# Two low parts of a tuned two-stack kernel, moved behind the fifth pair's maxima and the compressed softmax's first half

## The reference, cut to what matters

```python
def first_block(...):
    for l in range(DEPTH):                       # DEPTH = 2
        proj = h @ w_in[l]
        mixed = concat([nsa_mixer(...), gla_mixer(...), pool_mixer(...)])
        h = layer_norm(DEEPNORM_ALPHA * h + mixed @ w_out[l], ln1_g[l], ln1_b[l])
        ff = square(relu(h @ w_up[l])) @ w_down[l]
        h = layer_norm(DEEPNORM_ALPHA * h + ff, ln2_g[l], ln2_b[l])
```

## Time and profile before

| what | value |
|---|---|
| median of three runs | 1451.93 us |
| profiled execution, its own time | 1452.05 us |
| its span | 1450.3 us |
| TensorE busy | 1398.2 us, 96% of the span |
| VectorE busy | 1056.3 us, 73% |
| ScalarE busy | 833.0 us, 57% |
| GpSimd busy | 526.8 us, 36% |
| mean granted TensorE clock | 0.991 of full speed |

### The profile page before, as it was taken

One profiled execution on the slowest core, in us unless ns is written; L12 is line 12 of the kernel. 1 busy time (PEld: TensorE's weight loads), 2 busy tenths in 40 slices (PEclk: granted clock), 3 DMA queues, 4 the chain that ended last, 5 costly groups with the idle time before them and its releaser, 6 DMA issues.

```text
span 1450.3 us, 29999 instructions
## 1 busy us (share of the span) xinstructions
PE 1398.2 (96%) x12859; PEld 1182.3 (82%) x12859; DVE 1056.3 (73%) x1361; ACT 833.0 (57%) x1253; POOL 526.8 (36%) x421
## 2 busy tenths in 40 slices
PE   8999999999999999999999999999999999999997
PEld 6778888888778888878678788887777778888886
DVE  5897986567797874567786888766667765898853
ACT  5575554336664453456885665545566777575552
POOL 0143995131057990234211366401212202146620
PEclk9999999999999999999999999999999999999998
DMA  9434466545243665525235455552533233556550
GB/s 369 172 117 146 146 211 214 189 168 181 87 145 114 233 205 202 189 88 189 94 134 209 140 200 177 189 193 88 175 116 118 88 106 118 199 187 205 188 178 30
DMA packets 35717, 235.61 MB, mean 162 GB/s; under 512 B 4736, under 2 KB 6784, under 8 KB 8832
## 3 DMA queue, kind: packets, MB, share of 16 engines
q1 hardware_dynamic: 35584, 233.68, 46.9%
HBM read 232.62 MB, written 1.05 MB: 161 GB/s over the span
## 4 chain that ended last, share of the span: by engine, by line
PE 74%; DVE 15%; ACT 7%; issue 2%; DMA 2%; SPq 0%; DVEq 0%; ACTq 0%
PE psum L690 23%; PE psum L692 22%; PE psum L691 22%; DVE low L2144 4%; PE psum L778 2%; DVE arena L2534 2%; ACT high L1538 2%; DMA raw<-stream 2%; ACT m L1891 1%; DVE m L2602 1%; DVE arena L2254 1%; DVE arena L2605 1%; ACT arena L2028 0%; ACT L2025 0%; DVE u L2445 0%
## 5 line engine op out<-in xcount | busy, mean ns | idle before, releaser
L2144 DVE SCALAR_TENSOR_TENSOR low<-raw,high 128x2048 f16<-128x2048 f32 (+4 forms) x246 | 528.1, 2153 | 251.8 <-ACT high L1538 251.6
L690 PE MATMUL psum<-u,high 128*128 128x272 f16 (+3 forms) x2136 | 589.9, 276 | 14.8 <-DVE u L2445 5.5
L691 PE MATMUL psum<-u,high 128*128 128x272 f16 (+3 forms) x2136 | 589.5, 276 | 0.0
L692 PE MATMUL psum<-u,low 128*128 128x272 f16 (+3 forms) x2136 | 589.4, 276 | 0.0
L1538 ACT ACTIVATE high<-raw 128x2048 f16<-128x2048 f32 (+4 forms) x246 | 420.0, 1711 | 139.1 <-PE psum L692 125.7
L690 PE MATMUL psum<-arena,high 128*128 128x256 f16 (+2 forms) x1264 | 346.7, 274 | 2.8 <-ACT arena L1876 1.5
L691 PE MATMUL psum<-arena,high 128*128 128x256 f16 (+2 forms) x1264 | 346.6, 274 | 0.0
L692 PE MATMUL psum<-arena,low 128*128 128x256 f16 (+2 forms) x1264 | 346.6, 274 | 0.0
L690 PEld LDWEIGHTS psum<-u,high 128*128 128x128 f16 (+1 forms) x2136 | 210.0, 98 | 53.0 <-issue 15.7
L691 PEld LDWEIGHTS psum<-u,high 128*128 128x128 f16 (+1 forms) x2136 | 210.1, 98 | 31.2 <-issue 0.7
L692 PEld LDWEIGHTS psum<-u,low 128*128 128x128 f16 (+1 forms) x2136 | 210.0, 98 | 30.6
(11 more groups left out here) (331 smaller groups left out, 1498.7 us busy)
## 6 DMA issues: line engine op xcount, KB each, us to landing
raw<-stream SPq DMA_DIRECT2D x208, 1024.0 KB, 4.8
raw<-stream SPq DMA_DIRECT2D x8, 768.0 KB, 4.1
raw<-stream SPq DMA_DIRECT2D x3, 896.0 KB, 4.9
con<-consts SPq DMA_DIRECT2D x1, 1758.0 KB, 16.5
raw<-stream SPq DMA_DIRECT2D x3, 512.0 KB, 3.4
h<-x_t SPq DMA_DIRECT2D x2, 512.0 KB, 6.1
out_t<-h SPq DMA_DIRECT2D x4, 256.0 KB, 2.1
misc<-small SPq DMA_DIRECT2D x1, 512.0 KB, 13.3
```

What stands on the lines that cost most here:

```text
L690: pe.matmul(out, w_hi, x[0], start=start, stop=False)
L691: pe.matmul(out, w_hi, x[1], start=False, stop=False)
L692: return pe.matmul(out, w_lo, x[0], start=False, stop=stop)
L2144: tell(dve.scalar_tensor_tensor(low[:, at:at + w], raw[:, off:off + w], W_SCALE, high[:, at:at + w], ALU.mult, ALU.subtract), split_ready ...
```

## The change: what it does

Five calls of VectorE's program for a layer are reordered. Before: weigh(3), low_part(13), maxima(4), low_part(14), first half of the compressed softmax, weigh(4), maxima(5), second half, weigh(5), give(9). After: weigh(3), maxima(4), first half, weigh(4), low_part(13), maxima(5), second half, weigh(5), low_part(14), give(9). No other engine's program is changed, and no instruction changes its operands. Pairs are counted from 0, so maxima(4) are those of the fifth pair.

```diff
--- before.py
+++ after.py
@@ -2370,9 +2370,7 @@
                 tell(dve.scalar_tensor_tensor(h15, t15, 1.0, h15, ALU.add, ALU.mult), hid_gated)
                 give(8)
                 weigh(3)
-                low_part(matrices[f"cmp_{l}_0"] + SPLIT)
                 maxima(4)
-                low_part(matrices[f"cmp_{l}_1"] + SPLIT)
 
                 dve.wait_ge(cmp_scored, l + 1)
                 s15 = sc[:, :, 0:CMP_N]
@@ -2388,6 +2386,7 @@
                 tell.settle()
                 tell(dve.tensor_tensor(s15, s15, along(sc_s[:, 1, :], CMP_N), ALU.subtract), cmp_shifted)
                 weigh(4)
+                low_part(matrices[f"cmp_{l}_0"] + SPLIT)
                 maxima(5)
                 dve.wait_ge(cmp_exped, l + 1)
                 tell(dve.tensor_reduce(sc_s[:, 2, :], s15, AX_X, ALU.add))
@@ -2404,6 +2403,7 @@
                 tell.settle()
                 tell(dve.tensor_tensor(s15, s15, along(sc_s[:, 0, :], CMP_N), ALU.mult), cmp_ready)
                 weigh(5)
+                low_part(matrices[f"cmp_{l}_1"] + SPLIT)
                 give(9)
 
                 def gate_gla(i):
```

## The result

The changed kernel takes 1462.47 us (median of 6), the kernel before 1452.01 (6): ratio 1.0076, 95% interval 1.0065 to 1.0086, so 10.5 us slower. The profiled execution took 1467.02 us, the slowest of the six. A second profile of the same kernel, from an execution of 1464.61 us (experiment 1), stands beside it further down.

A forecast was written before the change was run, and what follows sets the result against it. TensorE holds 74% of the chain, VectorE 15%, with the operand chain ending 0.1 us ahead of TensorE; 1452.05 + 4.0 (layer 0) + 4.6 (layer 1) = 1460.65, median 1460.5, likeliest range 1458.4 to 1462.9, 8-in-10 range 1452.2 to 1464.5.

The forecast's parts named there:

- the likeliest case: Both layers: L2931 gets in ahead of gate_gla(0) at full clock; 1460.5 us, range 1458.4 to 1462.9, chance 0.62.
- the sum: Whole kernel: 1452.05 + 4.0 (layer 0) + 4.6 (layer 1) = 1460.65 us; median 0.12 lower, so 1460.5.
- The low parts themselves: Low parts 13 and 14 on VectorE, ending near 101 and 109: no wait for slots 13 and 14, cost nothing.
- Up to maxima(5): VectorE, layer 0: maxima(5) starts at 101.0 against 102.21, 1.2 us earlier; in layer 1 about 0.6 earlier.
- TensorE loses both waits: Layer 0: the waits for weigh(4) (0.88 us) and cmp_ready (0.50) vanish in the best case; pooled_out ends at about 109.8.
- Stretching beside GpSimd: VectorE beside GpSimd's pooling: at best low(13)'s extra 0.85 us disappears, at worst softmax and weighing take 1.3 us more.
- L2931 ahead of gate_gla(0): L2931, issued at about 109.8 during low(15), precedes gate_gla(0); the first L2413 lasts 3.8 us instead of 0.42.
- The prediction's limit of "about 112": Layer 0: L2931 misses gate_gla(0) only if issued after about 112, with TensorE later than before.
- The size of the collision: VectorE is stopped 3.4 us at gate_gla(0) per layer; by the skill page's wording, 2.2 us more per layer.
- Operand chain: From gate_gla(0) to the output product's tile 0: later by 4.0 us in layer 0, 4.6 in layer 1.
- TensorE waits in several pieces for L2170: TensorE waits for L2170 in several pieces, about 4 us, inside the first output pair.
- The clock: Rival 1: collision plus half clock in one layer, 1.7 to 3.4 us; about 1463, up to 1464.5, chance 0.16.

The follow-up runs named there:

- experiment 1: The changed kernel again, with no edit, for a second profile: 1463.43 us against 1452.35 for the kernel before, ratio 1.0074.
- experiments 2 and 3: L2931 as a memset, scaled residual left out: in the changed kernel 1454.58 us, ratio 1.0014; in the kernel before 1452.15 us, ratio 0.9996.
- Experiment 5: The changed kernel with GpSimd also waiting for gate_gla(1) before it issues L2931: 1457.27 us against 1451.85 for the kernel before, ratio 1.0036.
- 7: The kernel before with low(14) alone moved, from behind maxima(4) to behind weigh(5): 1460.97 us against 1451.85, ratio 1.0063.
- experiment 4: The changed kernel with 40 TensorE matmuls into an unused bank between values(5) and the output product: 1460.15 us, ratio 1.0050.

## Why the prediction was right, and where its sizes were off

Forecast 1460.5, measured 1462.47, in the range. The direction and the mechanism were those of the likeliest case, a collision of L2931 with the head of the operand chain. The range held with some luck, because the sum left out a term that the two profiles show at 3.5 and 4.0 us. By its steps:

- *The low parts themselves*: right. They end at 103.6 and near 111, and the product starts at 122.35. ScalarE's waits for raw loads sum to 13.2 us over the whole program, as before.
- *Up to maxima(5)*: from weigh(3) it was to start 11.0 us on (12.2 before). It took 12.4 in the first profile (103.50), whose scores(4) are late, and 10.1 in layer 0 of the second; in layer 1 12.1 and 12.3, where I expected 11.6. The step depends on when scores(4) arrive against weigh(3), and a single profile hid it.
- *TensorE loses both waits*: wrong. The wait for weigh(4) went. The one for cmp_ready grew from 0.50 to between 1.8 and 2.5, because TensorE got there 2 to 4 us earlier, while cmp_ready itself, which stands behind low(13) and maxima(5), came only 0.8 to 2.1 us earlier. pooled_out comes 0.1 to 0.8 us earlier against weigh(3), not 1.5. (The two waits sum to 1.38, so by its own figures the prediction had pooled_out end at 110.0 and not 109.8.)
- *Stretching beside GpSimd*: of the right kind. In the first profile low(13) took 2.82 instead of 3.13 and L2394 0.17 instead of 1.15, and others took longer instead (L2263 1.10 in layer 0, L2265 2.30 in layer 1). In layer 0 of the second L2394 is back at 1.15.
- *L2931 ahead of gate_gla(0)*: right in three of the four layers of two profiles, with 3.86 us against the 3.8 named; in the fourth L2415 was hit instead. That it is L2413 is partly luck. L2931 was to be issued 19.8 us after weigh(3) and came after 20.7 to 21.4. In layer 0 gate_gla(0) was to start after 20.9, so an L2931 at 21.4 would have missed it; in the first profile VectorE was late as well (22.3), and the two errors cancelled. The prediction's limit of "about 112" for a miss is too late for the same reason: by its own sum, anything after 110.9 misses L2413. The cost hardly depends on it, since the stop on L2415 moved the chain's end by 3.3 us, and the one on L2413 by as much beyond VectorE's own lateness (5.4 less 2.1 in layer 0 of the first profile).
- *The size of the collision*: experiments 2 and 3 together put 8.6 (11.08 less 2.43) of the 11.1 us of experiment 1 on L2931 beside the changed order (its work itself costs nothing in the old one). Experiment 5, with the work kept, gives 5.2 back, and its own lateness of VectorE hides how much more it would have given. So between half and four fifths of the loss is this collision with the clock's fall behind it, and 7 shows that it needs no part of low(13)'s move. The page of the Trainium skill that I weighed (SBUF — State Buffer, Who interferes with whom) has the port held for the whole instruction; L2931 lasted 6.21 us, 0.9 of it waiting for low(15), and the stop was 3.4. The rows were the better price.
- *Operand chain*: +4.0 and +4.6 forecast, 8.6 together. The chain's end moved by 5.4 and 5.0 us in the first profile (10.4) and by 3.3 and 5.2 in the second (8.5). That the second sum meets the forecast hides two errors, 0.7 too much in layer 0 and 0.6 too little in layer 1.
- *TensorE waits in several pieces for L2170*: wrong in form. It waits once, 3.5 to 4.8 us, because the first output tile needs the PSUM bank of the last projection tile, whose evacuation (L1524) stands behind the pool mixing in ScalarE's order. I had followed the operand and not the bank. The predicted wait inside the product shows only in experiment 4, at full clock.
- *The clock*: the mis-sized term. I gave the fall a case of its own with 0.16, in one layer, and left it out of the sum. It happened behind the wait in both layers of both profiles and cost 1.7 to 2.2 us each, 3.5 and 4.0 us per execution, and with the wait filled it was gone. The price named for it, 1.7 to 3.4 us, was right; the chance was not.

The two profiles are of executions slower than their kernel's median, with mean granted clocks of 0.986 and 0.988. The other eight executions of the changed kernel have 0.986 to 0.991, and 19 of the kernel before, beside experiment 1, have 0.991 to 0.994. So the fast ones lose some clock too, but how the median's 10.5 us split between chain and clock is not shown: both profiles add up to more.

## What to carry to other kernels

Where a long instruction of one engine can stop another engine, as L2931 stops VectorE here, an edit of either engine's order has to be followed to that instruction: a 3.4 us stop that is free on one instruction (L2170) costs its whole length, and the clock's fall with it, when it falls three or four instructions earlier (L2415 or L2413). Tie such an instruction down with a wait on what it must not overtake, before reordering around it. And ahead of a product, follow its first bank as well as its operand.

## What the runs showed of the hardware that I had not expected

- A waiting GpSimd instruction got in ahead of the next queued VectorE instruction in each of the rows shown (and in the changed kernel at 113.4 and 427.5), and VectorE was let in about 3.4 us later although GpSimd's record goes on for some 2 us more. The profile's spans of GpSimd are rough, so the record's end is weaker evidence than the 3.4 us on VectorE's side.
- A GpSimd memset of the same 128x2048 region took 1.80 us, and no VectorE instruction with two SBUF operands beside it was stretched (0.42 each, experiments 2 and 3).
- A TensorE wait of 3.5 to 4.8 us was followed by a granted clock at the lower level for most of the next 6 us or so (means of 0.58 and 0.60), while 40 matmuls of 256 columns in its place kept it at 1.00. A wait of 2.52 us for cmp_ready was followed by a fall in layer 0 of the second profile (0.58 from 104 to 106, 0.56 from 106 to 108) and by none in layer 1 of experiment 4 (1.00 from 416 to 422).
